# A gated linear attention scan: state kept as block diagonals of two heads, outputs of four heads in one PSUM bank, state updates by pairs of heads, and a modulation spread over twice as many turns

## The reference

```python
def gla_chunk_scan(q, k, v, log_a, s0):          # 4 heads, dk = 48, dv = 96
    def step(s, xs):                             # one chunk after the other
        b = jnp.cumsum(ac, axis=2)
        ...                                      # attn = masked q.k with decays
        o = jnp.einsum('bhid,bhde->bhie', qc * jnp.exp(b), s) + jnp.einsum('bhij,bhje->bhie', attn, vc)
        s_new = jnp.exp(b_last)[..., None] * s + jnp.einsum(
            'bhjd,bhje->bhde', kc * jnp.exp(b_last - b), vc)
        return s_new, o
# run forward and backward over the 256 context tokens, then over the 1024 latents from those states
sh1, sc1, g1, sh2, sc2, g2 = jnp.split(silu_c @ w_mod[l] + b_mod[l], 6)   # the modulation, 6 x 1024 columns
```

## Time and profile before

| | us |
|---|---|
| median of 3 runs | 4522.39 (4516.92 to 4524.83) |
| the profiled execution, its own time | 4524.4 |
| its span, first to last instruction | 4522.6 |
| the scan on PE, first to last matmul | 936.2 to 1129.5 |
| PE busy in the span | 4136.0 (91%) |
| mean granted TensorE clock in the span | 0.92 |

### The profile page before, as it was taken

The page is one execution under the profiler, slowest core; times in us unless marked ns, Lnnn a source line. Parts: engine busy times, 40 slices in busy tenths (PEclk is TensorE's granted clock), DMA queues, the critical chain, the costliest instruction groups (busy, mean ns, idle before and its releaser), DMA issues.

```text
span 4522.6 us, 51803 instructions
## 1 busy us (share of the span) xinstructions
PE 4136.0 (91%) x21422; PEld 2592.9 (57%) x21422; DVE 1522.0 (34%) x3393; ACT 946.0 (21%) x1822; POOL 608.2 (13%) x617
## 2 busy tenths in 40 slices
PE   6898998989889999999999899799989999799899
PEld 3477995656436644444444357686555547685454
DVE  2664553223334310111111372541054252631341
ACT  4122331121100020000000510321044310320341
POOL 3002330022001111000000310311000100311001
PEclk7996997965969899999999999999989999999899
DMA  5201102040234511111110130321100220311100
GB/s 195 88 3 29 27 18 92 24 142 1 94 124 161 186 37 37 37 37 46 38 37 33 38 121 19 89 61 55 33 33 24 79 85 28 103 42 56 42 24 37
DMA packets 215576, 278.18 MB, mean 62 GB/s; under 512 B 24429, under 2 KB 174152, under 8 KB 214448
## 3 DMA queue, kind: packets, MB, share of 16 engines
q1 hardware_dynamic: 201904, 206.17, 14.6%
q0 software_dynamic: 13440, 68.70, 4.0%
HBM read 240.03 MB, written 34.81 MB: 61 GB/s over the span
## 4 chain that ended last, share of the span: by engine, by line
PE 85%; DVE 7%; issue 3%; ACT 2%; DMA 2%; POOL 1%; SPq 0%; POOLq 0%; DVEq 0%; ACTq 0%
PE ps L789 15%; PE ps L2672 10%; PE ps L2686 10%; PE ps L2582 8%; PE ps L811 7%; PE ps L3341 6%; PE ps L3623 4%; PE ps L2340 2%; PE ps L3834 1%; PE ps L2384 1%; PE ps L3817 1%; PE ps L835 1%; DVE big L3436 1%; PE ps L1459 1%; PE ps L1443 1%
## 5 line engine op out<-in xcount | busy, mean ns | idle before, releaser
L789 PE MATMUL ps<-big 128*128 128x512 f32 (+1 forms) x1760 | 685.3, 550 | 14.2 <-DMA big<-hs_scratch 14.2
L789 PEld LDWEIGHTS ps<-big 128*128 128x128 f32 x1760 | 335.6, 192 | 353.6 <-issue 344.3
L2672 PE MATMUL ps<-big 128*128 128x512 f32 x1024 | 442.2, 594 | 8.6 <-issue 8.6
L2686 PE MATMUL ps<-big 128*128 128x512 f32 x1024 | 440.8, 592 | 0.0
L2582 PE MATMUL ps<-big 128*128 128x512 f32 (+1 forms) x896 | 359.3, 562 | 3.2 <-DVE big L3952 2.2
L2736 DVE SCALAR_TENSOR_TENSOR big<-ps,big 128x512 f32<-128x512 f32 x128 | 96.1, 751 | 776.6 <-PE ps L2686 776.6
L2672 PEld LDWEIGHTS ps<-big 128*128 128x128 f32 x1024 | 195.1, 191 | 254.2 <-issue 254.2
L2686 PEld LDWEIGHTS ps<-big 128*128 128x128 f32 x1024 | 194.6, 190 | 244.9 <-issue 244.9
L811 PE MATMUL ps<-big 128*128 128x256 f32 (+1 forms) x1792 | 319.2, 341 | 12.6 <-DVE big L1892 10.2
L811 PEld LDWEIGHTS ps<-big 128*128 128x128 f32 x1792 | 288.3, 194 | 43.9 <-DVE big L1892 10.3
L2582 PEld LDWEIGHTS ps<-big 128*128 128x128 f32 x896 | 169.6, 190 | 187.8 <-issue 182.2
(11 more groups left out here) (457 smaller groups left out, 5445.0 us busy)
## 6 DMA issues: line engine op xcount, KB each, us to landing
big<-in_w_mlp SPq DMA_DIRECT2D x32, 1024.0 KB, 5.3
big<-in_w_in SPq DMA_DIRECT2D x29, 1024.0 KB, 5.3
big<-in_w_mod SPq DMA_DIRECT2D x24, 1024.0 KB, 5.3
big<-in_w_ada SPq DMA_DIRECT2D x24, 1024.0 KB, 5.5
big<-us_scratch SPq DMA_DIRECT2D x72, 256.0 KB, 4.2
hs_scratch<-big POOLq DMA_DIRECT2D x3, 5120.0 KB, 15.1
big<-c_dft SPq DMA_DIRECT2D x12, 1024.0 KB, 5.2
xs_scratch<-big POOLq DMA_DIRECT2D x16, 640.0 KB, 3.8
```

Source lines behind the costliest of these rows:

```text
L789: t = e.matmul(b[:, 0:n], wv[:, k, 128 * m:128 * m + 128], K.hT[:, k, t0:t0 + n], start=(k == 0), stop=(k == 7))
L2672: t = e.matmul(b[:, :], wv[:, k, 128 * m:128 * m + 128], K.hT[:, k, t0:t0 + n], start=(k == 0), stop=(k == 7))
L2686: t = e.matmul(b[:, :], wv[:, k, 128 * m:128 * m + 128], h[:, k, t0:t0 + n], start=(k == 0), stop=(k == 3))
```

## The change

Four edits to `GlaScan` and one to the modulation's argument.

- The state is [128, 2, 192]: a pair's two heads as a block diagonal, zero off the blocks (the memset that clears it covers it all).
- The outputs of all four heads go to one bank. For each pair one matmul of all 128 rows by 192 columns gives `q @ state` for both heads, and two matmuls of 96 columns add `At @ v`.
- The state's update is one matmul for each pair, 128 weight columns by 192 columns. It also computes the products across heads, which nobody reads. DVE updates the four blocks one by one, 64 partitions each, where it took a pair at once.
- The outputs are copied or added by one instruction of 384 columns instead of two of 192.
- The modulation gets `gap` = 1: a round takes two turns (M in one, T in the next) where it took one (T of a round and M of the next in the same turn). It ends at turn 32 of 40, and ended at turn 17.

```diff
-        self.S, self.kdt = [H1.get(2, 96) for _ in range(2)], [H1.get(256) for _ in range(2)]
+        self.S, self.kdt = [H1.get(2, 192) for _ in range(2)], [H1.get(256) for _ in range(2)]
...
             if c < 8:
-                bs = [near[d][j].open(e, key(("o", j), d, c)) for j in range(2)]
+                u = key("o", d, c)
+                b = near[d][0].open(e, u)
...
-                for h in range(4):
-                    p, j = h // 2, h % 2
-                    i, o = slice(64 * j, 64 * j + 64), bs[j][:, 96 * p:96 * p + 96]
-                    e.matmul(o, m.At[d][:, j, 128 * p:128 * p + 128], m.vtm[:, c, 96 * h:96 * h + 96], start=True,
-                             stop=False)
-                    t = e.matmul(o, w["qs"][i, 256 * p + x:256 * p + x + 128], m.S[d][i, p, :], start=False, stop=True)
+                for p in range(2):
+                    e.matmul(b[:, 192 * p:192 * p + 192], w["qs"][:, 256 * p + x:256 * p + x + 128], m.S[d][:, p, :],
+                             start=True, stop=False)
+                    for j in range(2):
+                        o = slice(192 * p + 96 * j, 192 * p + 96 * j + 96)
+                        t = e.matmul(b[:, o], m.At[d][:, j, 128 * p:128 * p + 128], m.vtm[:, c, o], start=False, stop=(j == 1))
...
-            for h in range(4):
-                p, j = h // 2, h % 2
-                t = e.matmul(b[64 * j:64 * j + 64, 96 * p:96 * p + 96], m.kdt[d][:, 64 * h:64 * h + 64],
-                             m.vtm[:, c, 96 * h:96 * h + 96], start=True, stop=True)
+            for p in range(2):
+                o = slice(192 * p, 192 * p + 192)
+                t = e.matmul(b[:, o], m.kdt[d][:, 128 * p:128 * p + 128], m.vtm[:, c, o], start=True, stop=True)
...
-    later = Modulation(K, "later", A["w_mod"][0], 0, 16, 48, K.col("b_mod", 0, 48), K.modc, (7,))
+    later = Modulation(K, "later", A["w_mod"][0], 0, 16, 48, K.col("b_mod", 0, 48), K.modc, (7,), 1)
```

More of the change, by code:

```diff
@@ L1958, in split @@
         return x.rearrange("p (a c t) -> p a c t", a=2, c=2)
[L1960 to L1965, removed]
     def far(self, w):
@@ L2046, in second @@
                 e.wait_ge(*self.at("gla", "state", d, place - 1))
-                for h in range(4):
-                    p, j = h // 2, h % 2
-                    i, o = slice(64 * j, 64 * j + 64), bs[j][:, 96 * p:96 * p + 96]
-                    e.matmul(o, m.At[d][:, j, 128 * p:128 * p + 128], m.vtm[:, c, 96 * h:96 * h + 96], start=True,
-                             stop=False)
-                    t = e.matmul(o, w["qs"][i, 256 * p + x:256 * p + x + 128], m.S[d][i, p, :], start=False, stop=True)
-                    if p == 1:
-                        t.then_inc(P.sem, P.up(("mm", key(("o", j), d, c))))
+                for p in range(2):
[4 more added lines that the diff above has]
+                        t = e.matmul(b[:, o], m.At[d][:, j, 128 * p:128 * p + 128], m.vtm[:, c, o], start=False, stop=(j == 1))
+                t.then_inc(P.sem, P.up(("mm", u)))
             u = key("S", d, c)
@@ L2094, in second @@
             if 2 <= place <= 5:
[L2095 to L2099, removed]
+                u = self.key("o", d, c)
+                e.wait_ge(*self.at("mm", u))
+                e.activation(m.oacc[c], self.bank(u)[:, 0:384], ACT.Copy, scale=48 ** -0.5).then_inc(
+                    S.sem, S.up(("gla first", c), ("free", u, 0)))
         self.order(factors, first, second, [x.scalar_steps(e) for x in self.mods])
@@ L2138, in first @@
             if place > 2:
-                e.wait_ge(*self.at("mm", self.key(("o", 1), d, GDN_ORDER[d][place - 1])))
+                e.wait_ge(*self.at("mm", self.key("o", d, GDN_ORDER[d][place - 1])))
             for j in range(2):
@@ L2149, in second @@
                 e.wait_ge(*self.at("gla first", c))
[L2150 to L2154, removed]
+                u, o = self.key("o", d, c), m.oacc[c]
+                e.wait_ge(*self.at("mm", u))
+                e.scalar_tensor_tensor(o, self.bank(u)[:, 0:384], 48 ** -0.5, o, ALU.mult, ALU.add).then_inc(
+                    V.sem, V.up(("free", u, 0)))
             u = self.key("S", d, c)
@@ L2158, in second @@
             for p in range(2):
-                S = m.S[d][:, p, :]
-                e.scalar_tensor_tensor(S, S, m.dec[d][:, p, c:c + 1], self.bank(u)[:, 96 * p:96 * p + 96], ALU.mult,
-                                       ALU.add).then_inc(V.sem, V.up(("gla", "state", d, place), ("free", u, 0)))
+                for j in range(2):
+                    i, o = slice(64 * j, 64 * j + 64), 96 * j
+                    S = m.S[d][i, p, o:o + 96]
+                    e.scalar_tensor_tensor(S, S, m.dec[d][i, p, c:c + 1], self.bank(u)[i, 192 * p + o:192 * p + o + 96],
+                                           ALU.mult, ALU.add).then_inc(
+                        V.sem, V.up(("gla", "state", d, place), ("free", u, 0)))
         self.order(factors, first, second, [x.vector_steps(e) for x in self.mods])
```

## The result

The kernel after takes 4461.75 us (median of 4 runs, 4455.79 to 4463.91), the one before 4522.0 beside it (4 runs, 4516.92 to 4524.83): a ratio of 0.9866, with a 95% interval of 0.9849 to 0.9883. That is about 60 us less. The profiled execution took 4461.9 us. The page of after: span, granted clock in 40 slices, busy time.

What follows compares the result with a forecast made beforehand. PE, mostly at 0.50 clock, was taken to bound the scan: 125.5 us instead of 182.2, 56.7 less, minus 0.8 for DVE and 4 for half-clock units, 52 less. Forecast 4472.4 profiled, 4470 against the median; range 4455 to 4499.

Steps and rivals of the forecast that it cites:

- The likeliest case: Scan: PE's clock rises in place 2's outputs and holds but for stalls behind `factors`; 52 us less, 4460 to 4480, chance 0.57.
- Outputs and updates: PE in the scan: outputs plus update 4.27 us instead of 6.21 at half clock; 27.4 us less with the clock as before.
- the rule that spoke against this edit: State update on PE: column tiles of at most 64 give up to 2x; losing them would make the update 1.68 us.
- (b): PE's outputs and updates: 192 columns cost twice what 96 cost in this scan, 0.67 us; 28 us slower, chance 0.07.
- (c): PE's 192-column matmuls: weight load adds to the columns, 0.50 us each; 3 us slower, no change seen, chance 0.06.
- DVE's part: DVE's state updates: four of 64 partitions for two of 128; only the last shows, +0.46 us, plus 0.3 for memsets.
- The turns of the modulation: T and M in separate turns end PE's waits for L444 (4.1 us) and for `At` (5.1 us); 9.2 us less.
- no wait of L411 for L444: Sign in PE's waits: M no longer waits for L444, as it did 15 times before, 4.1 us.
- The stall behind `factors`: Places 3, 5 and 7: T and the outputs behind it wait for DVE and ACT; chains of 15, 15 and 16 us.
- The clock: PE's clock in the scan rises in place 2's outputs and holds but for stalls; 125.5 us instead of 182.2 from 947.3.
- two more units at half clock: Allowance in the scan's sum for some PE work still at half clock; 4 us taken off the gain.
- The rival that the clock stays as before: PE's clock in the scan stays mostly as it was; 36 us less, 21 if it never rises, chance 0.30.

Runs made afterwards that it cites:

- e1: The changed kernel with the modulation's gap back at 0, so outputs and updates alone; 4481.7 us, ratio 0.9911.
- e5: The kernel before with gap 1 and each direction's four `At @ v` ahead of its four `q @ state`, no block diagonal; 4457.9 us, ratio 0.9862.
- e6: The kernel before with only each direction's four `At @ v` put ahead of its four `q @ state`, gap 0; 4486.7 us, ratio 0.9927.
- e4: The changed kernel with `q @ state` in two matmuls of 96 columns instead of one of 192; 4460.2 us, ratio 0.9868.
- e8: The changed kernel with DVE's four state instructions reordered, those of the same partitions behind each other; 4448.1 us in one run.
- e2: The kernel before with only the modulation's gap set to 1; 4498.5 us, ratio 0.9949.
- e9: e8 with direction 1's factors moved behind `first(1)` of places 3, 5 and 7; 4448.1 us, ratio 0.9834.
- e11: The changed kernel plus 20 unread 96-column matmuls on PE behind `first(1)` of places 3, 5 and 7; 4453.1 us, ratio 0.9845.
- e10: e9 with the state updated by head, in four matmuls of 64 weight columns; 4439.7 us, ratio 0.9818.
- e7: e5 with direction 1's factors moved behind `first(1)` of places 3, 5 and 7; 4439.1 us, ratio 0.9822.
- e3: The changed kernel with the state updated by head, in four matmuls of 64 weight columns; 4455.2 us, ratio 0.9852.

## Why the prediction was right, and where it was not

The likeliest case happened: outputs without alternation, a clock that rises and holds but for three stalls behind `factors`. It was sized at 52 us less, and the stage gave 63.2; the time of 4461.75 us lies near the low end of that case's own range. The last matmul of the scan stands at 1062.6, where 1078 was expected. The 11 us more came mostly from a clock that rose in place 0, which no step of the prediction gives a reason for: that part is luck. By its steps:

**Outputs and updates.** Right. Outputs were to take 2.99 and 1.53 us, and took 3.07 and 1.59. 96 columns cost 0.20 and 0.10 an instruction (taken 0.214 and 0.111); 192 cost 0.345 to 0.39 and 0.18 to 0.20 (taken 0.32 and 0.16). The update was mis-sized: 0.68 to 0.78 us at full clock against 0.64, and 1.34 (e1, outputs behind it) to 1.56 (after, 946.49 - 944.93) at half clock against 1.28, on the way to the 1.68 of the rule that spoke against this edit. Rivals (b) and (c), at 0.67 and 0.50 for 192 columns, fell. That the alternation of rows was the cost is shown by e5 and e6, with the same 16 instructions in another order, and e4 rules out the order of accumulation. e5 and e6 also show what the prediction did not ask: whether the block diagonal was needed.

**DVE's part.** The state's four instructions take 1.34 us, not 1.0; 0.22 of it is their order on the partitions (e8). The tail behind the last update got 0.8 us longer, not 0.46; the last row of PE in the stage and the three that follow it in the chain of work:

```profile
1062.62 0.86 PE ps L2053 x4
...
1063.84 0.32 DVE big L2152
1064.16 0.03 issue
1064.19 0.30 DVE big L2152
...
1065.76 13.74 DMA big<-hs_scratch
```

**The turns of the modulation: right as a sum of waits, with the clock left out.** 9.2 us was taken from the waits of before, to be gone. Net, the waits that went are 7.0 us with the turns alone (e2) and 8.0 beside the faster outputs (e1 to after). But "no wait of L411 for L444" did not come true: that wait is 9.2 us in after. And the turns gave 22.6 us of the stage alone and 24.6 on top of e1, because the clock rose with them. The prediction put the rise on the outputs and nothing on the turns. e2, which keeps the alternation, has 37.5 us at 1.00 (17.1 in before); e6, which ends it and keeps the turns as they were, 34.1; e5, with both, 73.2.

**The stall behind `factors`.** Right in place, engine and nearly in size, but that M stalls there too was not foreseen: from the update of direction 0 to the outputs behind T it was to take 15, 15 and 16 us. It took 979.74 - 963.32 = 16.4, again 16.4, and 15.9.

**The clock.** Right in direction. Two terms were too cautious. I had the clock rise in the outputs of place 2; it rose at 948.9, in place 0. So the rest of place 0 and place 1 took 11.7 us, not 14.9, and place 2 up to its first update 6.7, not 12.0: 8.5 us. And 4 us for two more units at half clock did not occur. With 1.5 of hand-overs that were not there, less 2.7 for three chains that took longer, this makes 11.3 us, which is the distance between 52 and 63.2. Why the clock rose that early is open. It is not the alternation: places 0 and 1 have no outputs, and before stayed at 0.50 there. What differs there between the kernels is the update and the turns. In all six traces with the update by pair (after, e1, e4, e8, e9, e11) the clock rose 4.8 to 5.0 us behind the start of the stage, with the turns or without. With the update by head and the turns it was 4.9 (e10), 8.6 to 8.9 (e2, e5, e7) and 18.7 us (e3); with neither, 39.5 (e6) and 63.4 (before). Behind place 2 the time at 1.00 does not rank the kernels with one trace each: e5 (73.2 us) has one change of rows in its outputs, where after (93.0), e3 (64.4), e4 (84.0), e8 (75.3) and e10 (74.5) have none. The rival that the clock stays as before, 36 less, fell, though it was right that it would fall at each of the three stalls. The Trainium skill ("TensorE: Matmul & The Clock Gate", What's actually happening) says that activity releases the clock and idling throttles it; the trace agrees: after's windows at 0.50 begin within the stalls that end at 978.87 and 1009.57, and at 1034.2 between one of 3.04 and one of 3.64 us, and e11 supports it. e7's last window, at 0.50 with PE busy 21.43 of 22.90 us, is not explained by it.

## What to carry to other kernels

Look at the tile shapes in the order in which PE issues them before changing the work: where matmuls of different rows alternate, putting those of one shape behind each other gave here the same time as a block diagonal, at the cost of two loops. When an engine becomes faster, walk the chain of the engines beside it again from its new pace: waits of 9.2 us before were 32.0 beside the faster outputs (e1), and moving one piece of DVE and ACT work by a place was worth 12.0 us of the stage (e7 against e5), a fifth of the whole change. When an edit removes waits, look at where they go, and read PE's busy time with the same instructions apart from its waits: most of what the turns gave stood in the busy time. A stall of PE can have two prices, the stall itself and a half-speed stretch behind it; here the stalls of T were the larger (10.4 us, e9 against e8) and the stretches some 6.4 (e11), by one trace each.

## What was unexpected of the hardware

- Six changes between 128 and 64 rows fewer save 3.12 - 1.66 = 1.46 us at full clock: 0.24 each. At half clock e6's outputs took 3.05 us and before's 5.37, so 0.39 each. A part of it is that 64-row instructions go faster behind each other: 0.62 / 8 = 0.078 us each in e5, with 1.04 / 8 = 0.13 for those of 128 rows.
- The Trainium skill ("TensorEngine Tiling (Array Packing)", Theoretical Speedup) gives up to 2x for tiles of at most 64 columns. The traces show 0.48 us for the update by head and 0.68 to 0.78 by pair: 1.4x to 1.6x, but some 0.1 goes into the change of tile before it and 0.1 into the one between it and T (e3).
- A DVE instruction of 64 partitions by 96 costs 0.34 us in after where each is on other partitions than the one before, 0.28 in e8, while one of 128 partitions by 96 cost 0.27. Half the partitions are no cheaper here.
- PE's clock can stay at 0.50 with PE busy for 94% of 22.9 us (e7), and be 1.00 with PE busy for 75% of 27.3 us (after's first window). What held it down in e7 is open.
